# In both attentions TensorE takes every second unit's steps in reverse order

## The reference

```python
# first block: 8 heads of 64, chunks of 64 queries that see their own and 8 earlier chunks
scores = einsum('bcqhd,bckhd->bhcqk', qc, kb) * HEAD_DIM ** -0.5 + bias
probs = softmax(where(valid, scores, NEG_INF)); out = einsum('bhcqk,bckhd->bcqhd', probs, vb)
...
# second block: 16 heads of 64 over 4 key groups; a "selected" and a "window" branch (and compressed blocks o_c)
p_s = masked_softmax(s_s, dist_s >= 0); o_s = einsum('bgqhk,bgqkd->bqghd', p_s, v_g)
p_w = masked_softmax(s_w, m_w);         o_w = einsum('bgqhk,bkgd->bqghd', p_w, vw_b)
out = g0 * o_c + g1 * o_s + g2 * o_w
```

## Time and profile before

| what | value |
|---|---|
| median of 3 runs | 2275.35 us (2271.84 to 2278.64) |
| the profiled execution's own time | 2273.31 us |
| its span, first to last instruction | 2271.5 us |
| granted TensorE clock, mean over the span | 0.995 |
| TensorE (PE) busy | 2185.8 us, 96% |
| GpSimd (POOL) busy | 1210.4 us, 53% |
| VectorE (DVE) busy | 1160.8 us, 51% |
| ScalarE (ACT) busy | 775.4 us, 34% |
| first attention on TensorE | about 143 to 186 us |
| second attention on TensorE | about 1370 to 1519 us |

### The profile page before, as it was taken

The page is one execution under the profiler, slowest core; times in us unless marked ns, Lnnn a source line. Parts: engine busy times, 40 slices in busy tenths (PEclk is TensorE's granted clock), DMA queues, the critical chain, the costliest instruction groups (busy, mean ns, idle before and its releaser), DMA issues.

```text
span 2271.5 us, 40259 instructions
## 1 busy us (share of the span) xinstructions
PE 2185.8 (96%) x16188; PEld 1723.7 (76%) x16188; DVE 1160.8 (51%) x1715; ACT 775.4 (34%) x1355; POOL 1210.4 (53%) x678
## 2 busy tenths in 40 slices
PE   6999999999999999989989998999999999999999
PEld 3867877888888667778867565668887777888887
DVE  7984647555510467744444526672227537555500
ACT  5464223333310266533324226761002232323200
POOL 1964453788877200000006445567787357777776
PEclk9999999999999999999999999999999999999999
DMA  8443652332322322220002240002233212323223
GB/s 329 139 158 123 239 185 87 113 101 93 100 95 92 133 90 74 78 76 5 4 4 93 75 158 11 2 11 93 94 102 128 93 39 92 102 92 97 97 93 102
DMA packets 64768, 220.75 MB, mean 97 GB/s; under 512 B 6897, under 2 KB 9082, under 8 KB 64626
## 3 DMA queue, kind: packets, MB, share of 16 engines
q1 hardware_dynamic: 50448, 179.81, 24.1%
q10 hardware_dynamic: 9986, 24.82, 3.0%
q0 software_dynamic: 4192, 14.06, 1.8%
HBM read 213.09 MB, written 11.86 MB: 99 GB/s over the span
## 4 chain that ended last, share of the span: by engine, by line
PE 76%; POOL 8%; issue 7%; DVE 7%; ACT 1%; DMA 1%; DVEq 0%; POOLq 0%; SPq 0%; ACTq 0%
PE banks L497 13%; PE banks L499 12%; PE banks L498 12%; POOL WH L450 4%; PE banks L2001 3%; POOL WL_A L453 3%; PE banks L1956 3%; PE banks L668 2%; PE banks L684 2%; PE banks L721 2%; PE banks L880 2%; PE banks L882 2%; PE banks L881 2%; PE banks L2237 2%; PE banks L2238 2%
## 5 line engine op out<-in xcount | busy, mean ns | idle before, releaser
L450 POOL TENSOR_TENSOR WH<-W,ZERO 128x1024 fp32r<-128x1024 f32 x194 | 371.1, 1913 | 286.0 <-PE banks L499 253.3
L453 POOL TENSOR_TENSOR WL_A<-W,WH 128x1024 fp32r<-128x1024 f32 x138 | 339.4, 2459 | 10.8
L497 PE MATMUL banks<-HF,WH 128*128 128x512 f32 x704 | 275.9, 392 | 1.3 <-DVE HF L2964 1.3
L498 PE MATMUL banks<-HF,WH 128*128 128x512 f32 x704 | 273.9, 389 | 0.0
L499 PE MATMUL banks<-HF,WL_A 128*128 128x512 f32 x704 | 273.9, 389 | 0.0
L487 POOL TENSOR_TENSOR WH<-W,ZERO 128x1024 fp32r<-128x1024 f32 x20 | 41.1, 2057 | 280.3 <-DVEq L398 202.0
L847 POOL TENSOR_TENSOR WR_LO<-W,FRONT_HI 128x1024 fp32r<-128x1024 f32 x40 | 95.9, 2402 | 128.1 <-ACT FRONT_HI L841 84.8
L497 PEld LDWEIGHTS banks<-HF,WH 128*128 128x128 f32 x704 | 132.1, 188 | 29.2 <-DVE HF L2964 1.7
L498 PEld LDWEIGHTS banks<-HF,WH 128*128 128x128 f32 x704 | 132.1, 188 | 27.6 <-issue 0.2
L499 PEld LDWEIGHTS banks<-HF,WL_A 128*128 128x128 f32 x704 | 132.1, 188 | 27.6
L453 POOL TENSOR_TENSOR WL_C<-W,WH 128x1024 fp32r<-128x1024 f32 x56 | 141.4, 2526 | 4.4
(11 more groups left out here) (489 smaller groups left out, 5275.0 us busy)
## 6 DMA issues: line engine op xcount, KB each, us to landing
W<-stream SPq DMA_DIRECT2D x308, 512.0 KB, 3.5
BIG<-stream ACTq DMA_DIRECT2D x30, 512.0 KB, 5.0
BIG<-stream SPq DMA_DIRECT2D x24, 512.0 KB, 11.0
bias_rows<-bias_lines POOLq DMA_DIRECT2D x1, 4096.0 KB, 22.7
BIG<-bias_rows POOLq DMA_DIRECT2D x1, 2816.0 KB, 14.2
X<-x_t SPq DMA_DIRECT2D x2, 1024.0 KB, 7.4
bias_rows<-bias_lines POOLq DMA_DIRECT2D x1, 2048.0 KB, 16.6
BIG<-bias_rows POOLq DMA_DIRECT2D x1, 2048.0 KB, 11.8
```

What stands on the lines that cost most here:

```text
L450: nc.gpsimd.tensor_tensor(WH[:, half, :], W[:, slot, :], ZERO[:, 0:1].to_broadcast([P, D]), ALU.add)\
L453: nc.gpsimd.tensor_tensor(WL[stage][half], W[:, slot, :], WH[:, half, :], ALU.subtract)\
L497: nc.tensor.matmul(out_ap, w_hi, hi, start=start, stop=False)
L498: nc.tensor.matmul(out_ap, w_hi, lo, start=False, stop=False)
```

## The change

TensorE's loop takes its three steps in reverse order in every odd round from the fifth on: O(*i*−4), T(*i*−3), S(*i*). Even rounds keep S, T, O. So two units' outputs follow each other, and two units' scores. In the same odd rounds VectorE copies the turn *i*−3 ahead of the maxima of unit *i* instead of behind them. No instruction is added or removed; no semaphore and no buffer changes. The bodies of the steps become local functions, which moves line numbers (scores stay L668; turns L684 → L682; outputs L721 → L717; VectorE's maxima L769 → L782, copies L800 → L792, reciprocals L781 → L803).

```diff
@@ pe_pairs
-            for i in range(n + SUM):
-                if i < n:
-                    u = units[i]
...
-                if TURN <= i < n + TURN:
-                    j = i - TURN
...
-                if i >= SUM:
-                    j = i - SUM
...
+            for i in range(n + SUM):
+                back = i > SUM and i % 2 == 1
+                if i < n and not back:
+                    scores(i)
+                if i == 1 and first is not None:
+                    first(pe)
+                if back:
+                    outputs(i - SUM)
                 if TURN <= i < n + TURN:
+                    turn(i - TURN)
                 if blocks is not None and 6 <= i < 10:
                     pe_block_turn(pe, i - 6)
+                if i < n and back:
+                    scores(i)
+                if i >= SUM and not back:
+                    outputs(i - SUM)
@@ dve_pairs
+            def copy(j):
+                w = units[j]["width"]
+                dve.wait_ge(p_tr, 2 * (a0 + j) + 2)
+                if j >= 2:
+                    dve.wait_ge(p_pv, a0 + j - 1)
+                nc.vector.tensor_copy(PT[stage][j % 2][1][:, 0:w], psum[5][:, 0:w]).then_inc(p_pt[1], 1)
+
             for i in range(n + SUM + 2):
+                if TURN <= i < n + TURN and i > SUM and i % 2 == 1:
+                    copy(i - TURN)
                 if i < n:
                     scores(i, 0)
...
-                if TURN <= i < n + TURN:
-                    j = i - TURN
...
+                if TURN <= i < n + TURN and not (i > SUM and i % 2 == 1):
+                    copy(i - TURN)
```

More of the change, by code:

```diff
@@ L658, in pe_pairs, with scores, turn @@
             a0, n = BASE[stage].pair, len(units)
-            for i in range(n + SUM):
-                if i < n:
-                    u = units[i]
[L662 to L673, removed]
+            def scores(i):
+                u = units[i]
+                for c in range(2):
+                    if i >= 2:
+                        pe.wait_ge(p_max, 2 * (a0 + i - 2) + c + 1)
+                    elif blocks is not None:
+                        pe.wait_ge((b_act, b_dve)[i], 2)
+                    for part in u["parts"]:
+                        last = nc.tensor.matmul(psum[2 * (i % 2) + c][:, part["at"]], part["q"][c], part["k"][c],
+                                                start=True, stop=True)
+                    last.then_inc(p_sc, 1)
+            def turn(j):
+                if j == 0:
                     pe.wait_ge(v_c, VALUES[stage])
@@ new lines, in outputs @@
+            def outputs(j):
+                u = units[j]
+                bank = psum[6 + u["pair"] % 2]
+                if u["first"]:
+                    if u["pair"] >= 2:
+                        for done in p_out:
+                            pe.wait_ge(done, BASE_OUT[stage] + u["pair"] - 1)
+                    if blocks is not None and u["pair"] < 2:
+                        if u["pair"]:
+                            pe.wait_ge(b_act, 8)
+                        for c in range(2):
+                            nc.tensor.matmul(bank[DH * c:DH * (c + 1), :], con("ident", lo=0, hi=32)[:, DH:2 * DH],
+                                             con("scan", lo=0, hi=32), start=True, stop=False)
+                    elif blocks is not None:
+                        for c in range(2):
+                            v, p = blocks(u["pair"], c)
+                            nc.tensor.matmul(bank[DH * c:DH * (c + 1), :], v, p, start=True, stop=False)
+                if blocks is not None and j in LATE_BLOCKS:
+                    pe.wait_ge(v_c, 4 + 4)
+                    pe.wait_ge(b_act, 8)
+                    for c in range(2):
+                        v, p = blocks(LATE_BLOCKS[j], c)
+                        nc.tensor.matmul(psum[6 + LATE_BLOCKS[j]][DH * c:DH * (c + 1), :], v, p, start=False,
+                                         stop=(LATE_BLOCKS[j] != u["pair"]))
+                for copied in p_pt:
+                    pe.wait_ge(copied, a0 + j + 1)
+                for part in u["parts"]:
+                    n_b, b0 = part["nk"] // P, part["at"].start // P
+                    closes = blocks is None or u["last"] and u["pair"] > 0 and part is u["parts"][-1]
+                    for b in range(n_b):
+                        for c in range(2):
+                            last = nc.tensor.matmul(bank[DH * c:DH * (c + 1), part["cols"]], part["v"][c][b],
+                                                    PT[stage][j % 2][c][:, (b0 + b) * P:(b0 + b + 1) * P],
+                                                    start=(blocks is None and b == 0), stop=(b == n_b - 1 and closes))
+                last.then_inc(p_pv, 1)
```

55 lines of the change are left out of this document (8 added, 47 removed).

## The result

The changed kernel takes 2310.56 us (median of 3 runs, 2307.01 to 2315.32) against 2275.35: a ratio of 1.0164 over the runs, 95% interval 1.0146 to 1.0182 (the quotient of the two medians alone is 1.0155). It is slower, and inside the range of the prediction (2285 to 2316), 10 us above its middle. The profiled run took 2307.01 us, with a span of 2305.2 against the earlier trace rows.

A forecast was written before the change was run, and what follows sets the result against it. TensorE was taken as the bound, to be replaced by a chain through VectorE's late copy: 8.5 (`attend1`) + 16 (`attend2`'s steady part) + 1.8 (its opening) = 26 us on 2273.3, giving 2300 us; range 2285 to 2316.

The forecast's parts named there:

- my case: Whole kernel: VectorE's late copy makes a chain that slows both attentions; 2293 to 2308 us, 60 in 100.
- the clock's rival: TensorE's clock falls in the new stalls, once per `attend2` period and twice in `attend1`; 2308 to 2320 us, 16 in 100.
- the opening: Start of `attend2`: unit 5's scores, and block work with them, come later; adds 1.8 us, bounds 0 and 2.
- What bounds the kernel: Both attentions: paced by TensorE's own groups before the change, with every copy, maximum and exponential in time.
- the point that decides: After S(i), VectorE needs four maxima and a copy, 3.5 us for B and C, against 2.7 of TensorE work.
- the outputs of F and of D: Fourth and sixth of `attend2`'s six-unit period A to F: TensorE stalls mostly ahead of these, 1.6 to 1.7 us each.
- the first rival: Both attentions: copies are in time and joined groups pay, 8.9 us saved, 2264 us; 6 in 100.
- The chain: `attend2`'s steady part: VectorE and TensorE wait on each other in turn; 19.3 us per six units against 17.07, 16 in all.
- What joined groups save: Both attentions: the second of two like groups loses its fixed part, 0.20 us for scores, 0.15 for outputs; 8.9 in all.
- The first attention: `attend1`: the same chain in its middle plus 4.5 us at its end; adds 8.5 us, bounds 5 and 11.
- Passed on in full: Behind each attention: the next stage starts from its last outputs, so both delays reach the total whole.

The follow-up runs named there:

- e8: Changed kernel, but reversed only in `attend2` from round 13 to the last scores, with VectorE's and ScalarE's copies moved early; 2274.46 us, 0.9991 of the kernel before.
- e10: Changed kernel, but reversed only in `attend2` and from round 7 on instead of 5; 2296.41 us, 1.0089 of the kernel before.
- e4: Changed kernel, but reversed in `attend1` only, `attend2` as before the change; 2289.49 us, 1.0065 of the kernel before.
- e12: Changed kernel, but only round 5 of `attend2` reversed, on TensorE and VectorE, all else as before; 2281.78 us, 1.0021 of the kernel before.
- e1: Changed kernel, but VectorE takes both maxima of a unit ahead of the previous unit's reciprocals; 2309.44 us, 1.0160 of the kernel before.
- e6: Changed kernel, but reversed only in `attend2` and only from round 13 on, behind the opening; 2296.44 us, 1.0081 of the kernel before.
- e9: Changed kernel, but reversed in `attend1` only, and there only in rounds that still have scores (5 to 11); 2289.52 us, 1.0046 of the kernel before.
- e11: e8 with reversed rounds ending at 45 instead of 47 and, in round 15, the first pair's output copy ahead of the early copy; 2275.06 us, 0.9987.

## Why the prediction was right, and what it mis-sized

*The number.* The forecast for the profiled execution was 2300, and 2307.01 came: at the upper end of what the bounds of the terms gave (2285 to 2307). The median, 2310.56, lies above my case (2293 to 2308), where I had put the clock's rival (2308 to 2320), and is in the range because the range took in half of that case. Two of the three terms were outside their own bounds: `attend1` 12.2 for 5 to 11, the opening 7.2 for 0 to 2; 4.8 us came back that I had not counted on. So the mechanism earned the direction and most of the size, and the exact place in the range is in part luck.

*What bounds the kernel, and the point that decides.* Right. TensorE lost its place as the bound at exactly the two places named, the outputs of F and of D: 1.71 and 1.61 us forecast as 1.6 to 1.7, 13 times for 14 to 16. With the copies in time (e8) TensorE is the bound again, as the first rival had it, with 0.73 saved in a period for 1.05, so that rival was refuted for the order as changed, not for joined groups as such.

*The chain.* Forecast 19.3, measured 20.17. VectorE's three links, from its first maximum to the outputs, are 4.38 (1472.90 to 1477.28), 3.52 and 3.74: 11.64. Less the reciprocals' waits, 0.91 and 0.23, that is 10.5, against 9.69 and 0.45 of handing over. The waits are 1.1 against 1.0; most of the rest is VectorE's own busy time, 11.67 in a period where the sum took the 11.35 of before. TensorE's links, from those outputs to VectorE's next maximum, are the other 8.5 (2.99 the first, 1469.91 to 1472.90), against 8.25 − 0.3 + 0.27: the 0.3 taken off for joined outputs was wrong, because an output that has waited starts afresh. O(F) takes 1.02 and O(D) 0.80, no less than in the earlier trace rows. Each error is small; all went the same way.

*What joined groups save.* Forecast 1.05 in a period, measured 0.73: the scores nearly as forecast (0.52 for 0.6), the outputs 0.24 for 0.45. The fixed part of a group was read rightly: A and B, whose copies are there in good time, save all of an output's 0.15. What is missing is missing where a copy still comes just in time, at D and F. The Trainium skill's "TensorEngine Tiling (Array Packing)", Key Properties, has TensorE drain at a change of tiling mode; e8 agrees that something is saved where such changes fall away, 0.1 to 0.2 us at each place where no copy is waited for.

*The opening.* Forecast 1.8, measured 7.2; this is the largest miss, and the term of the sum that was mis-sized most. The mechanism was right: GpSimd's scaling starts at 1401.22 instead of 1388.73, 2.3 later once the 10.2 brought along are taken off. What I left out is what follows: in the wait of 4.03 the clock fell, for 6.82 us, and the later block turns wait as well (e10). No run separates the clock's share.

*The first attention.* Forecast 8.5, measured 12.2. Up to unit 6 it was 4.8 with one half-clock stretch in it, from there to the end 7.4 with another. The two stretches can have cost 1.7 us each, 3.4 of the 3.7 missing. No run was made with the clock held, but e4, the same order in `attend1`, prices the first of them by about 1.5: its own first stretch lies at 151.94, ahead of the outputs, and from unit 0 to unit 6 its lateness grows by 3.7 (0.9 to 4.5) instead of 5.2. That stretch need not come from the change: e8 and e12, which leave `attend1` as it was, have one near 151 too, and their unit 0 is 1.0 and 0.5 late. ScalarE copied turn 10 later than I said (near 186), and the last outputs wait for its next copy:

```profile
189.78 0.49 ACT L755 ACTIVATE BIG<-banks 128x384 f32<-128x384 f32 x1 [3.01 <-PE banks L682]
...
195.94 0.57 ACT L755 ACTIVATE BIG<-banks 128x512 f32<-128x512 f32 x1
```

*The clock.* As a rival it had one fall for each period of `attend2` and two in `attend1`. Two came in `attend1` (the first perhaps not by the change) and one in the opening; in the steady part none did: no stretch from 1409.40 to the end of the attention is below 1.00, with 13 waits of up to 1.7 us. The Trainium skill's "TensorE: Matmul & The Clock Gate", section "A second HAM failure mode: psum-queue depth-cycling", which has the clock swing when TensorE idles shortly between groups often enough, doesn't show at these stalls. The prediction's "1.00 through attentions" holds for their middles: the kernel before has stretches at 0.50 at the end of `attend1` (184.13, 3.41 us) and in the opening of `attend2` (1375.38, 6.83 us).

*Passed on in full.* Nearly: VectorE's work near 990 us is 12.5 late where the last outputs of `attend1` were 12.2; 2.0 us came back between the attentions, all of it in the recurrent mixer behind 990, where executions differ most (last section), and 2.8 behind the second.

The sum was 26 us on 2273.3 and the profiled run gave 33.7: +3.7 in `attend1`, −2.0 between, +5.4 in the opening, +3.1 in the steady part, −2.8 behind.

## What to carry to other kernels

Before putting two like steps next to each other, walk the other engines' queues from the moment that each step's input is there: joining S(*i*) with S(*i*+1) handed VectorE two units' work in front of one copy, and a chain that closes through a queue sets the period whatever the bound engine saves. A late copy has a second one behind it on another engine, and behind that a store that nobody needs yet; only when all three had been moved did the saving appear, and it was 0.7 of 17 us, with the copies still only just in time. A stall is priced by the wait and by the clock that may fall behind it.

## What the runs showed of the hardware that I had not expected

In `attend1` the granted clock fell to 0.50, the 1.2 GHz level, in an idle 1.27 us that ended at 156.93 (TensorE had been busy 3.57 of the 6.70 us before) and behind a wait of 2.24 that ended at 179.28, in `attend2`'s steady part behind none of 13 waits of up to 1.7; the length of one stall doesn't tell. And the recurrent mixer between the attentions, which no run here changed, is where executions differ most: the stretch at half clock near its end, about 1180, lasted 3.41 us before, 6.83 in the changed kernel, and in four of the experiments (e1, e6, e9, e11) 20.48:

```profile
1184.24:1187.65 3.41, 3.41 (x5) 1.35 (x4) 3.31 (x4) 1.10 (x3) 2.07 (x1) 0.50 0.01 2
```

```profile
1177.49:1197.97 20.48, 15.99 (x224) 10.71 (x220) 8.16 (x12) 2.83 (x5) 4.24 (x2) 0.50 0.01 2
```

The first is the kernel before, the second e11, whose lateness grew by 10 us from the end of `attend1` to the first outputs of `attend2`. By the same VectorE instructions in both, 5.1 of them had come at 1166 (a time of the kernel before), ahead of the long stretch, and 3.7 more at 1180, with it; the other three runs with a long stretch lost 3.6 to 4.1 between these two points. At 990 us every run is still within 1.4 of the lateness of its last outputs in `attend1`. A single profile of this kernel can't show a gain of 4 us in its total; the lateness inside a stage can.
